# Weighting and summing the two expert rows of a token on TensorE instead of VectorE, and waiting for a block's stores one round later

## The reference

```python
y_slot = yb[dest] * wts.reshape(-1)[order][:, None].astype(x.dtype)
return jax.ops.segment_sum(y_slot, tok, num_segments=n_tok)
...
x = x + gate2 * ffn.reshape(bsz, L, D_MODEL)
```

## Time and profile before

| what | value |
|---|---|
| median of three runs | 1698.69 us (1693.38 to 1699.51) |
| the profiled execution, its own time | 1698.96 us |
| its span, first to last instruction | 1697.4 us |
| busy: PE, DVE, ACT, POOL | 85%, 32%, 17%, 7% of the span |
| mean granted TensorE clock | 0.926 of full |
| last copy of a block's result starts | 1649.21 us |
| first weighting operation of the tail starts | 1664.55 us |

### The profile page before, as it was taken

The page is one execution under the profiler, slowest core; times in us unless marked ns, Lnnn a source line. Parts: engine busy times, 40 slices in busy tenths (PEclk is TensorE's granted clock), DMA queues, the critical chain, the costliest instruction groups (busy, mean ns, idle before and its releaser), DMA issues.

```text
span 1697.4 us, 46436 instructions
## 1 busy us (share of the span) xinstructions
PE 1450.0 (85%) x20310; PEld 1107.3 (65%) x20311; DVE 545.1 (32%) x1104; ACT 283.0 (17%) x498; POOL 124.1 (7%) x195
## 2 busy tenths in 40 slices
PE   5999899867887699999995697899999989998760
PEld 3677689746776566667443575677778767786540
DVE  4916860257778641211235000011110101100006
ACT  2213000232222310000011111111111111111112
POOL 0060300100000000000002000000000000000002
PEclk9999896577999799999996799999999999999995
DMA  8286421530311011114118899878880975349974
GB/s 347 87 249 241 80 47 51 193 118 27 112 63 50 1 38 50 63 49 174 38 37 331 308 394 404 312 291 300 300 317 25 339 297 216 123 161 396 403 307 185
DMA packets 87175, 319.20 MB, mean 188 GB/s; under 512 B 11056, under 2 KB 11312, under 8 KB 86864
## 3 DMA queue, kind: packets, MB, share of 16 engines
q1 hardware_dynamic: 72288, 270.05, 42.0%
q0 software_dynamic: 14832, 48.34, 9.4%
HBM read 283.46 MB, written 32.80 MB: 186 GB/s over the span
## 4 chain that ended last, share of the span: by engine, by line
PE 69%; DVE 11%; DMA 11%; SPq 3%; issue 2%; ACT 2%; POOL 1%; POOLq 0%; DVEq 0%; ACTq 0%
PE ps L1765 20%; PE ps L1389 14%; PE ps L1750 9%; DMA expert_w<-in_w_up 8%; PE ps L1704 4%; PE ps L1668 4%; PE ps L1615 3%; PE ps L1553 2%; PE ps L1518 2%; DMA weight_ring<-in_stream 2%; PE ps L1401 2%; SPq L466 2%; PE ps L1572 1%; PE ps L1733 1%; SPq L472 1%
## 5 line engine op out<-in xcount | busy, mean ns | idle before, releaser
L1765 PEld LDWEIGHTS ps<-x_block_t,expert_w 128*64 128x64 f32 x14336 | 455.1, 139 | 176.3 <-issue 98.8
L1765 PE MATMUL ps<-x_block_t,expert_w 128*64 128x64 f32 x14336 | 461.0, 224 | 51.6 <-DMA expert_w<-in_w_up 50.2
L1389 PE MATMUL ps<-h_t,weight_ring 128*128 128x320 f32 x1024 | 283.2, 437 | 3.6 <-ACT h_t L625 3.6
L1389 PEld LDWEIGHTS ps<-h_t,weight_ring 128*128 128x128 f32 x1024 | 196.9, 193 | 91.1 <-issue 13.5
L1332 DVE TENSOR_TENSOR act_t<-silu_tmp,ps 128x64 f32<-128x64 f32 x224 | 49.5, 221 | 590.5 <-ACT silu_tmp L786 590.5
L1750 PE MATMUL ps<-expert_w,act_t 128*64 128x512 f32 x896 | 229.5, 599 | 0.0
L786 ACT ACTIVATE silu_tmp<-ps 128x64 f32<-128x64 f32 x224 | 50.2, 224 | 585.4 <-PE ps L1765 585.4
L1615 PE MATMUL ps<-node_x 128*128 128x128 f32 x560 | 73.7, 290 | 28.9 <-DVE att L1115 14.8
L1615 PEld LDWEIGHTS ps<-node_x 128*128 128x128 f32 x560 | 69.2, 201 | 33.8 <-DVE att L1115 17.1
L1704 PE MATMUL ps<-w_out_sb,merged 128*128 128x512 f32 x160 | 69.3, 593 | 1.7 <-DVE merged L1215 1.7
L574 POOL DMA_DIRECT2D y_sorted<-y_block x56 | 30.3, 541 | 515.2 <-DVE y_block L1336 513.4
(11 more groups left out here) (306 smaller groups left out, 1342.7 us busy)
## 6 DMA issues: line engine op xcount, KB each, us to landing
expert_w<-in_w_gate SPq DMA_DIRECT2D x128, 512.0 KB, 14.0
expert_w<-in_w_up SPq DMA_DIRECT2D x128, 512.0 KB, 14.9
expert_w<-in_w_down SPq DMA_DIRECT2D x128, 512.0 KB, 14.9
weight_ring<-in_stream SPq DMA_DIRECT2D x98, 512.0 KB, 5.0
x_sorted<-zero POOLq DMA_DIRECT2D x18, 512.0 KB, 18.8
x_block<-x_sorted POOLq DMA_DIRECT2D x29, 256.0 KB, 6.5
y_sorted<-y_block POOLq DMA_DIRECT2D x56, 128.0 KB, 5.1
y_sorted<-zero POOLq DMA_DIRECT2D x9, 512.0 KB, 29.2
```

Of the source, the lines that this page charges most:

```text
L1389: last = mm(pair(job)[:, a, :], w[:, k, :], h_t[:, k, a * HALF:(a + 1) * HALF], start=(k == 0), stop=(k == KD - 1))
L1765: last = mm(ps[cols, 2 * w + f % 2, 0:MB], w_slot[3 * f + w][:, k, cols], x_blk_t[:, k, :], start=(k == 0), stop=(k == KD - 1))
```

## The change

The first two operations of DVE for a chunk go to PE. A tile `w_diag` of ten diagonal 128x128 matrices is made by one DVE operation ahead of the block loop, one matrix for each chunk and each of the two experts, with the tokens' weights on the diagonal. In the tail PE forms for each chunk diag(w0) x got[2c] + diag(w1) x got[2c+1] in PSUM, in two halves of 512 columns, so four float32 matmuls of 128x128 by 128x512. The chunks take turns on two pairs of PSUM banks. DVE multiplies the sum, which it reads from PSUM, by the gate row, and adds the residual; two of its four operations are left.

The wait of POOL for the stores of a block moves to the next round, behind the load of the next block's rows; one wait stands behind the loop. So that the counts fit without a first grant, two of the DMAs that zero `y_sorted` early in the kernel count on `y_stored` instead of `zeroed`.

```diff
+        w_diag = at("weight_diag", ring0 + 16384, [P, 2 * CH, P])
...
-        ZEROED = 16 * (X_ROWS // P + (OVER * MB + P - 1) // P)
+        ZEROED = 16 * (X_ROWS // P + (OVER * MB + P - 1) // P - 2)
...
-                    .then_inc(zeroed, 16)
+                    .then_inc(zeroed if r < Y_ROWS - 2 * P else y_stored, 16)
 
             pool.wait_ge(zeroed, ZEROED)
+            pool.wait_ge(y_stored, 32)
...
             pool.sem_inc(y_copied, 1)
-            pool.sem_inc(y_free, 1)
...
                     pool.dma_start(x_blk[0:MB, :], x_sorted[bass.ds(i * MB + MB, MB), :]).then_inc(x_blk_in, 16)
 
+                    pool.wait_ge(y_stored, i * 32 + 32)
+                    pool.sem_inc(y_free, 1)
                     pool.wait_ge(y_copied, i + 2)
                     for half in range(2):
                         pool.dma_start(y_sorted[bass.ds(i * MB, MB), 512 * half:512 * half + 512],
                                        y_blk[MB * half:MB * half + MB, :]).then_inc(y_stored, 16)
-                    pool.wait_ge(y_stored, i * 32 + 32)
-                    pool.sem_inc(y_free, 1)
                 pool.nop()
             pool.wait_ge(x_blk_in, blocks * 16 + 16)
+            pool.wait_ge(y_stored, blocks * 32 + 32)
...
+            vec.tensor_tensor(w_diag[:, :, :], bc(ident, 1, 2 * CH), bc(rt[:, N_GS, 20:30], 2, P), ALU.mult)\
+                .then_inc(w_diag_ready, 1)
...
-            w_of = rt[:, N_GS, 20:30]
             for c in range(CH):
                 cv = 0 if c < SCH else 1
-                dve.wait_ge(got_in[c], 32)
-                done(vec.tensor_scalar(got[2 * c][:, :], got[2 * c][:, :], w_of[:, c:c + 1], None, ALU.mult))
-                done(vec.scalar_tensor_tensor(got[2 * c][:, :], got[2 * c + 1][:, :], w_of[:, 5 + c:6 + c],
-                                              got[2 * c][:, :], ALU.mult, ALU.add))
-                done(vec.tensor_tensor(got[2 * c][:, :], got[2 * c][:, :], g2_row[:, cv, :], ALU.mult))
-                vec.tensor_tensor(fin[c][:, :], got[2 * c][:, :], x2[:, c, :], ALU.add).then_inc(x3_ready, 1)
+                dve.wait_ge(summed, c + 1)
+                vec.tensor_tensor(fin[c][:, :].rearrange("p (a n) -> p a n", a=2), ps[:, 2 * (c % 2):2 * (c % 2) + 2, :],
+                                  g2_row[:, cv, :].rearrange("p (a n) -> p a n", a=2), ALU.mult).then_inc(sum_took, 1)
+                dve.wait_ge(sum_took, c + 1)
+                vec.tensor_tensor(fin[c][:, :], fin[c][:, :], x2[:, c, :], ALU.add).then_inc(x3_ready, 1)
                 if c >= 1:
                     final(c - 1)
...
+            pe.wait_ge(w_diag_ready, 1)
+            for c in range(CH):
+                pe.wait_ge(got_in[c], 32)
+                if c >= 2:
+                    pe.wait_ge(sum_took, c - 1)
+                for half in range(2):
+                    for j in range(2):
+                        last = mm(ps[:, 2 * (c % 2) + half, :], w_diag[:, CH * j + c, :],
+                                  got[2 * c + j][:, 512 * half:512 * half + 512], start=(j == 0), stop=(j == 1))
+                last.then_inc(summed, 1)
```

More of the change, by code:

```diff
@@ L296, in hybrid_step @@
         got_in = [sem(f"got_in{s}") for s in range(CH)]
+        w_diag_ready = sem("w_diag_ready")
+        summed = sem("summed")
+        sum_took = sem("sum_took")
         c_ready = sem("c_ready")
```

## The result

The median of 20 runs is 1687.41 us (1669.18 to 1697.42) against 1695.72 us of the kernel before (1682.09 to 1707.14, 20 runs). The medians are 8.3 us apart, and over all runs the means are 8.0 us apart (1686.8 against 1694.8). The ratio is 0.9944, with a 95% interval of 0.9916 to 0.9972: 9.5 us faster (4.7 to 14.2). Ratios in this document leave out, as a slower state, runs over 1.5% above the fastest of their kernel, which here are four of the 20 after (1695.09 us and above) and none of before, so that this ratio shows the change as larger than the means of all runs do. The forecast was 4.35 us.

What follows compares the result with a forecast made beforehand. It took the wait chain from the last block's copy, then DVE in the tail, to bound what the change touches; -1.95 + 0.4 - 2.8 = -4.35 us gave 1694.3 us from a median of 1698.69, range 1688 to 1704.

Steps and rivals of the forecast that it cites:

- moved wait: At the block loop's end, POOL's empty rounds run while the stores land: -1.95 us, bounds 0 and -2.49.
- matrices beside the scatters: Ahead of the block loop, the DVE operation making the diagonal matrices stretches a POOL scatter: +0.4 us, bounds 0 and 0.74.
- tail: After the gathers, two DVE operations per chunk go to PE: 27.0 us against 29.79, so -2.8 us.
- so the rounds start at 1651.69: At the loop's end, empty rounds begin after the second store's issue of 0.54 us; first gather at 1655.98.
- so from the median of 1698.69 I forecast 1694.3 us: Whole kernel: the -4.35 us sum applied to the median of three earlier runs, 0.26% faster.
- the 5.2 us of the forecast: In the tail, PE's full clock returns 5.2 us after its first matmul, so chunk 0 takes 6.0 us.
- The lower bound of 4.2 us: Shortest time for PE's clock to return in the tail, from work begun at 1013.8; chunk 0 then 5.4 us.
- the slower rival: PE's clock does not come back in the tail: +8.8 us, 1707.5 us; chance 0.09, including low for three chunks.
- what cannot be hidden is chunk 0 and most of chunk 1: In the tail, DVE's 3.9 us per chunk hides PE's matmuls only from chunk 2 on.
- the 65 ns that the prediction estimated: In the tail, the skill's extra PSUM read cost per DVE operation, 0.3 us over five chunks; not borne out by the trace.
- the bound of 0.74: Ahead of the loop, upper bound in us on the scatter's stretch: longest gather 1.706 over the median 0.964.
- the fourth rival: In the block loop, row loads fall beside stores and weight stream: +9.6 us, 1704 us; chance 0.12 for several us either way.

Runs made afterwards that it cites:

- e4: The whole change timed once more against the kernel before: ratio 0.9968 (0.9936 to 1.0001), 5.4 us faster; 42.8 us from last copy to end of span.
- e9: Kernel before with 28 rounds in POOL's loop instead of 35, so no empty rounds: last copy to first gather 5.61 us.
- e10: Kernel with only POOL's wait for the stores moved, and 28 rounds in POOL's loop instead of 35: last copy to first gather 5.31 us.
- e5: Whole change, but DVE makes the diagonal matrices only after the last scatter has landed: ratio 0.9961 (0.9930 to 0.9991) against the kernel before, longest scatter 1.36 us.
- e3: Kernel before plus only the weighted sum on PE with its diagonal matrices, wait for stores at its old place: ratio 0.9994 (0.9957 to 1.0031), tail 26.86 us.
- e6: On top of e5, PE multiplies constants, five unused float32 products, while the first gathers are under way: ratio 0.9970 against the kernel before, tail 24.04 us.
- e8: Whole change with every product of the sums made twice, 80 matmuls instead of 40: tail 42.91 us, DVE's chunks 6.87 us apart.
- e1: The kernel before, unchanged, timed against itself: ratio 1.0035 (1.0007 to 1.0064); 48.5 us from last copy to end of span.
- e7: Kernel before plus the DVE operation that makes the diagonal matrices, unused: longest scatter 1.99 us, first scatter to first transposes 24.4 us.

## Why the prediction was right and wrong

**The size, by its terms.** The mechanism and the sign were right, and the two terms that bring time were sized too low; the third came near by luck.

| term | forecast, us | measured, us |
|---|---|---|
| moved wait | -1.95 (0 to -2.49) | -2.55 |
| matrices beside the scatters | +0.4 (0 to +0.74) | 0.99 at the scatters; +0.4 by means behind them, not shown |
| tail | -2.8 | -3.3 (mean of 26.08, 26.86, 26.89, 26.32 against 29.83) |
| sum | -4.35 | -5.45 |

With the sum of the last column the ratio would be 0.9968, which is what the repetition (e4) gave; with 0 or 1.0 in place of the 0.4 that is not shown, the sum is -5.85 or -4.85. The first ratio, 0.9944, holds 4 us more, of which more below. The forecast of 4.35 us lies just outside its interval, whose end on that side is 4.7.

**The step that failed**, of those that give the gain, is the start of the empty rounds: "so the rounds start at 1651.69", with the reason "since POOL's queue runs in order". The trace after shows the first of them at 1640.19, at the moment at which the second store's issue begins (1639.70 + 0.49); what takes POOL 0.54 us for a store does not hold up its sequencer, which only counts rounds. The end of the range that was called the bound, -2.49 us, is what happens: the term was -1.95 us and measured -2.55. e9 and e10 show that no more than 0.3 us of it is anything but this overlap.

The absolute time failed at another step, "so from the median of 1698.69 I forecast 1694.3 us": the level of the kernel before was taken from three runs, and over 20 runs it is 1695.72, 3.0 us lower. The two terms mis-sized are the moved wait, by 0.6 us, and the tail, by 0.5 us. Of the 6.9 us between 1694.3 and the measured 1687.4, these are 3.0 us and the terms 1.1 us; the other 2.8 us are taken up under the spread.

**The tail.** DVE's share of a chunk is 3.79 us, not 3.9; three chunks make 0.3 of the 0.5 us. The clock came back 4.1 us behind the first matmul in the first profile, 4.6 in e5, 5.7 in e3 and 5.8 in e4, so the 5.2 us of the forecast are inside what it does. The tails of these four, 26.08, 26.32, 26.86 and 26.89 us, follow it at half a microsecond for each microsecond. The lower bound of 4.2 us is close to the earliest of them by luck: it was read from work that began at 1013.8, and there the clock was still at 1.00, as the row shown says. The windows behind it, from 1014 and from 1015, have 0.81 and 0.50, so the clock fell only then, in the middle of the work, and was back at about 1018.0. That the clock does not come back, the slower rival, was seen in none of the profiles with matmuls in the tail. The prediction's own formula, by which what cannot be hidden is chunk 0 and most of chunk 1, held: DVE waits for PE twice. The price of reading PSUM was nothing, 1.22 us for 1024 columns as from SBUF, against the 65 ns that the prediction estimated from the Trainium skill's page "VectorE: DVE Perf Modes" (section on the TRN2 errata).

**The scatter.** That the means give the forecast 0.4 us is luck, for the row behind it was misread. The scatter of 1.36 us was taken as stretched by a third of the 1.29 us of DVE beside it. The row merges two operations of 0.69 us; the scatter began 0.18 us into the first and ended 0.85 us behind the end of that one, as the others of the 51 do. So it had been held to the end of that operation in full. By that reading one operation of 1280 columns holds a scatter longer, as it did, for 1.0 us, outside the bound of 0.74. Here the rule of the Trainium skill ("SBUF — State Buffer", section "Who interferes with whom"), blocked until the other is done, was nearer: the scatter started 0.37 us behind the start of the DVE operation and ended 0.82 us behind its end, close to a whole issue of 0.95 us after it. e5 takes the delay away by moving the operation.

**The loop.** It is 702.5 us on average in the five profiles without the moved wait (703.2, 702.6, 702.8, 702.1, 702.0) and 701.5 in the seven with it (701.6, 704.4, 700.8, 701.5, 700.4, 701.4, 700.7); e9 and e10 are among them, since they leave out empty rounds only. Whether a microsecond is gained there stays open; the collision that the fourth rival spoke of, +9.6 us, is not there.

**The spread.** The rest of the measured difference was not a term of the change. The same program has medians of 1693.38 to 1695.72 us in the larger sets, so the range, built around 1698.69, ended too high at its low end; from 1695.7 the forecast of 4.35 us would have been 1691.4. What the ratio of 0.9944 holds beyond the terms is not told from noise. With every run counted the means differ by 8.0 us in the first comparison, by 7.0 in the second (e4 against all 47 runs of the kernel before) and by 6.2 in the third (e5), each with a standard error of 2.0 to 2.4 us; 5.45 us is within about one of each. That the runs spread with the clock is shown: over 71 runs of the kernel before with the clock on record, the three shortest (1677 to 1678 us) have a mean granted clock of 0.935 to 0.937, and the 14 above 1700 us one of 0.918 to 0.924. Of where in the kernel, the profiles show the one early stretch, with up to 20 us; other stretches have not been followed up, though the one behind it, 605 to 607 us in the others, was 608 to 611 us in e4, e6, e8 and e10.

## What to carry to other kernels

A wait for stores that stands in front of cheap control work, such as the empty rounds of a loop with a fixed count, cost its landing once here; place it directly before the first use of the data, and count the overlap from the issue, not from the end of the engine's busy time. Work that was moved to an idle TensorE started at the lower clock in each of the five profiles with nothing ahead of it: cost its first microseconds from rows at that clock, and keep the engine busy through the wait ahead of it if the first result is waited for (2.3 us of the tail, e6 against e5). A row that merges several operations must be taken apart before a stretch of time beside it is read as a share. When executions spread by more than the effect, take the marks of each stage from several profiles and compare stage with stage, and time the kernel against itself before believing an interval.

## What was not expected of the hardware

The same code of a stretch in which PE never pauses took 58.3 us at a granted clock of 1.00 and 77.6 us at 0.71, and which of them an execution gets changes from one to the next. PE's row reads busy for the whole stretch in both. An indirect DMA's issue of 0.95 us on POOL became 1.94 to 1.99 us beside one DVE operation of 1.49 us with two inputs in SBUF. Whether such an issue is slow hangs on the moment of its start: all 51 that began inside an operation of this kind ended 0.81 to 0.85 us behind its end. So the two gathers of 1.7 us of the kernel before are 1.02 us at most in e1 and e7, with the same operations of DVE in the tail, where they began at other points of them.
